# A low-half subtraction moved from VectorE to GpSimd, with the steps around it three to five picks later

## The reference, cut to what matters

```python
def chunk(xc):                                   # 128 tokens at a time
    qc = (xc @ w_query).reshape(C, PEER_HEADS, 2, half)
    s = jnp.einsum('chpd,hpnd->chpn', qc, sub_keys)
    top_s, top_i = lax.top_k(s, PEER_TOPK)       # 16 of 128, twice per head
    ...                                          # 16 of their 256 sums
    u = expert_u[expert_idx]                     # rows of 2048 floats
    vv = expert_v[expert_idx]
    act = jax.nn.gelu(jnp.einsum('chkd,cd->chk', u, xc))
    return jnp.einsum('chk,chkd->cd', (g * act).astype(vv.dtype), vv)
```

## Time and profile before

| | |
|---|---|
| median of 3 runs | 1889.43 us (1888.48 to 1889.85) |
| profiled execution | 1888.83 us, span 1887.1 us |
| PE busy | 1282.0 us (68%) |
| VectorE busy | 1343.8 us (71%) |
| ScalarE busy | 377.1 us (20%) |
| GpSimd busy | 807.5 us (43%) |
| HBM read | 631.29 MB, 337 GB/s over the span |

### The profile page before, as it was taken

How to read it: one execution, slowest core, us unless ns; L and a number is a source line. 1 busy time by engine, 2 the same in 40 slices (tenths; PEclk the granted TensorE clock), 3 DMA queues, 4 the chain that set the end, 5 groups by cost and what they waited for, 6 DMA issues and landing times.

```text
span 1887.1 us, 12624 instructions
## 1 busy us (share of the span) xinstructions
PE 1282.0 (68%) x3739; PEld 691.2 (37%) x3739; DVE 1343.8 (71%) x1811; ACT 377.1 (20%) x642; POOL 807.5 (43%) x539
## 2 busy tenths in 40 slices
PE   4799999989866667656555555655565555555567
PEld 3688887777644434211111111111121111111122
DVE  3354556355559989787787877878787787878764
ACT  3233442443422121111110101011011110101001
POOL 1000010000003655665665656666655666665654
PEclk8899999989888889877877778777777777777779
DMA  7666644415429999999999999999999999999998
GB/s 171 196 190 189 186 138 127 142 61 207 156 88 406 413 421 418 421 421 422 421 422 422 417 421 405 419 417 420 421 413 411 422 414 422 419 407 422 422 422 355
DMA packets 129230, 636.22 MB, mean 337 GB/s; under 512 B 13762, under 2 KB 22564, under 8 KB 63124
## 3 DMA queue, kind: packets, MB, share of 16 engines
q0 software_dynamic: 75136, 540.58, 70.0%
q1 hardware_dynamic: 54036, 94.95, 15.4%
HBM read 631.29 MB, written 4.19 MB: 337 GB/s over the span
## 4 chain that ended last, share of the span: by engine, by line
DMA 43%; PE 33%; DVE 8%; POOL 7%; issue 6%; ACT 2%; POOLq 0%; SPq 0%; DVEq 0%; ACTq 0%
DMA big<-in_peer_expert_v,pick_row 27%; DMA big<-in_peer_expert_u,pick_row 13%; PE ps L1443 11%; PE ps L1159 6%; PE ps L1160 6%; PE ps L1161 6%; POOL big L420 5%; DVE big L1078 3%; DMA raw<-in_w_in 2%; POOL big L415 2%; DVE split_lo L647 1%; PE ps L1226 1%; DMA raw<-in_peer_w_query 1%; PE ps L1146 1%; DVE ht L675 1%
## 5 line engine op out<-in xcount | busy, mean ns | idle before, releaser
L1443 PE MATMUL ps<-big,diag 128*128 128x512 f32 x1024 | 706.1, 828 | 491.2 <-DMA big<-in_peer_expert_v,pick_row 439.4
L1078 DVE CUSTOM_DVE_ANT_0 big<-big 128x2048 f32<-128x2048 f32 x256 | 586.2, 2291 | 212.1 <-DMA big<-in_peer_expert_u,pick_row 210.8
L420 POOL DMA_INDIRECT big<-in_peer_expert_v,pick_row x256 | 448.1, 1751 | 391.1 <-PE ps L1443 291.2
L1443 PEld LDWEIGHTS ps<-big,diag 128*128 128x128 f32 x1024 | 225.9, 243 | 960.1 <-DMA big<-in_peer_expert_v,pick_row 716.3
L415 POOL DMA_INDIRECT big<-in_peer_expert_u,pick_row x256 | 339.8, 1327 | 180.7 <-issue 70.4
L1096 DVE SCALAR_TENSOR_TENSOR big<-big,pick_w 128x1024 f32<-128x1024 f32 x256 | 327.5, 1279 | 47.8 <-DMA big<-in_peer_expert_v,pick_row 46.4
L647 DVE TENSOR_TENSOR split_lo<-raw,split_hi 128x1024 fp32r<-128x1024 f32 x152 | 185.7, 1223 | 197.8 <-ACT split_hi L444 167.6
L1159 PE MATMUL ps<-split_hi,ht 128*128 128x512 f32 x608 | 248.4, 409 | 73.9 <-DVE split_lo L647 73.9
L610 ACT ACTIVATE diag<-ident,pick_w 128x128 f32<-128x128 f32 x256 | 95.3, 395 | 808.0 <-PE ps L1443 489.1
L1160 PE MATMUL ps<-split_lo,ht 128*128 128x512 f32 x608 | 241.6, 397 | 0.0
L1161 PE MATMUL ps<-split_hi,ht 128*128 128x512 f32 x608 | 241.2, 397 | 0.0
(11 more groups left out here) (193 smaller groups left out, 677.2 us busy)
## 6 DMA issues: line engine op xcount, KB each, us to landing
raw<-in_w_in SPq DMA_DIRECT2D x88, 512.0 KB, 4.6
raw<-in_w_out SPq DMA_DIRECT2D x32, 512.0 KB, 3.5
raw<-in_peer_w_query SPq DMA_DIRECT2D x32, 512.0 KB, 11.1
raw<-in_cmp_k_w SPq DMA_DIRECT2D x8, 512.0 KB, 4.0
raw<-in_cmp_v_w SPq DMA_DIRECT2D x8, 512.0 KB, 4.1
big<-in_peer_expert_u,pick_row POOLq DMA_INDIRECT x256, 11.5
big<-in_peer_expert_v,pick_row POOLq DMA_INDIRECT x256, 11.4
big<-in_x SPq DMA_DIRECT2D x2, 1024.0 KB, 5.9
```

The source lines that it names most:

```text
L420: pool.indirect_dma_start(ring[g % RING], None, v_table, bass.IndirectOffsetOnAxis(pick_row[:, m - LAG:m - LAG + 1], 0)).then_inc(gathered ...
L1078: dve.tensor_tensor_reduce(row, row, XN[:, m // (PICKS // TT), :], 1.0, 0.0, ALU.mult, ALU.add, pick_dot[:, m:m + 1]).then_inc(dotted, 1)
L1443: ins = pe.matmul(psf[:, t * V_PE + c:t * V_PE + c + 512], diag[:, m % DIAGS, :], row[:, c:c + 512], start=k == 0, stop=k == PICKS // TT - 1)
```

## The change

GpSimd makes the low halves of query chunks 1 to 3, at k = 4 to 11, ahead of the pick's gathers. ScalarE's high halves move from k = 0..7 to 3..10, TensorE's products from 0..7 to 5..12. `to_q` moves from 9 to 13, `turn_chunk` from 10 to 13, `queries_turned` from 11 to 14, `chunk_scores` from 12 to 14 and `scores_out` from 14 to 15. The low halves of all other weights and of chunk 0 stay on VectorE.

```diff
@@ gpsimd
+            def lo(c, s):
+
+                pool.wait_ge(hi_done, SP_QUERY + c * STEPS_PER_CHUNK + s + 1)
+                pool.tensor_tensor(split_lo[:, s % SPLIT, :], raw[:, s % RAW, :], split_hi[:, s % SPLIT, :].bitcast(F32),
+                                   ALU.subtract).then_inc(split_done, 1)
+
             for m in range(STEPS):
+                n, k = divmod(m, TOPK)
+                if n + 1 < W_CHUNKS and 4 <= k < 4 + STEPS_PER_CHUNK:
+                    lo(n + 1, k - 4)
                 if m < PICKS:
                     g = u_place(m)
@@ scalar
-                    if k < STEPS_PER_CHUNK:
-                        hi_steps(c * 2 + RAW_QUERY // RAW, c * STEPS_PER_CHUNK + SP_QUERY, k, k + 1)
-                    if k == 11:
+                    if 3 <= k < 3 + STEPS_PER_CHUNK:
+                        hi_steps(c * 2 + RAW_QUERY // RAW, c * STEPS_PER_CHUNK + SP_QUERY, k - 3, k - 2)
+                    if k == 14:
                         queries_turned(c)
@@ vector
-                    if k < STEPS_PER_CHUNK:
-                        lo(k % RAW, SP_QUERY + c * STEPS_PER_CHUNK + k)
-                    if k == 9:
+                    if k == 13:
                         to_q(c)
-                    if k == 14:
+                    if k == 15:
                         scores_out(c)
@@ tensor
-                    if k < STEPS_PER_CHUNK:
-                        gemm_step([ps[:, 4 + t, :] for t in range(TT)], k % SPLIT, (2 * k, 2 * k + 1), CHUNK,
-                                  SP_QUERY + c * STEPS_PER_CHUNK + k)
-                    if k == 10:
+                    s = k - 5
+                    if 0 <= s < STEPS_PER_CHUNK:
+                        gemm_step([ps[:, 4 + t, :] for t in range(TT)], s % SPLIT, (2 * s, 2 * s + 1), CHUNK,
+                                  SP_QUERY + c * STEPS_PER_CHUNK + s)
+                    if k == 13:
                         turn_chunk(c)
-                    if k == 12:
+                    if k == 14:
                         chunk_scores(c)
```

## The result

The changed kernel takes 1961.33 us (median of 4 runs, 1960.78 to 1961.87) against 1888.95 us for the kernel before beside it: ratio 1.0386, 95% interval 1.0368 to 1.0404. It is 72 us slower. I had forecast 13 us slower and a range up to 1922 us. The profiled execution has a span of 1960.1 us, 73.0 more than before.

What follows compares the result with a forecast made beforehand. The prediction took the DMA engines to bound the pick loop, with VectorE hidden behind them. Losses of 9.0 (chunk 1) + 0 (chunk 2) + 3.8 us (chunk 3) made 12.8 us, giving 1902 us; range 1887 to 1922 us.

Steps and rivals of the forecast that it cites:

- the ceiling on any gain: Loop over the picks: DMA engines are nearly always full, so relieving an engine gives back at most 4.1 us; 0 taken.
- The duration of the subtraction: GpSimd's subtraction over 1024 columns: 2.05 us taken as two passes, with bounds of 1.1 and 3.0 us.
- The port: SBUF access: GpSimd's subtraction is shut out while VectorE works on two SBUF operands; the reverse direction not shown by rows.
- Chunk 1: Picks 4 to 11: rounds of subtraction and gather take 5.2 us, so the twelfth gather starts 9.0 us late.
- a closer coupling: ScalarE's split waits for same-pick matmuls of s - 2: 5.7 us a pick, under 6.23 in chunk 2; cost 0.
- GpSimd's round in chunks 2 and 3: Two gathers, gaps, subtraction and half a dot: 6.83 us a pick, costing 0 in chunk 2 and 3.8 us in chunk 3.
- The queue of 6.0 us as cover: In front of the DMA engines: about 6.0 us of transfers are normally queued, so GpSimd may be late by that much.
- The score steps at 0: Squeezed turn of the queries: VectorE waits some 2.3 us in chunk 1, less later, covered by queued rows; cost 0.
- The lower clock: Rival: TensorE falls to the lower clock in chunks 2 and 3, about 1947 us, or 1914 with half the picks; chance 0.07.

Runs made afterwards that it cites:

- Experiment 7: Changed kernel with products and high halves three picks earlier and GpSimd clearing the low half twice instead of subtracting: 1889.57 us, ratio 1.0007.
- experiment 2: Changed kernel, but GpSimd clears the low half twice instead of subtracting, reading nothing from SBUF, with place and wait kept: 1945.46 us, ratio 1.0308.
- experiment 3: Chunk 1 as in the changed kernel, chunks 2 and 3 as in the kernel before: 1895.37 us, ratio 1.0045.
- experiment 4: Changed kernel with products and high halves three picks earlier, GpSimd's subtractions unchanged: 1913.68 us, ratio 1.0130.
- experiment 8: All steps at the changed places, VectorE making the low halves; GpSimd only waits for the high half at the same place: 1947.52 us, ratio 1.0313.
- experiment 9: Kernel before with only the score steps at their changed later places, split and products as before: 1887.49 us, ratio 0.9997.
- experiment 1: Changed kernel with all steps at the changed places, but VectorE makes the low halves and GpSimd has no part: 1895.03 us, ratio 1.0041.
- both experiments: Changed kernel with products and high halves one pick earlier, 1928.49 us; changed kernel with GpSimd subtracting behind the pick's gathers, 1931.57 us.

## Why the prediction was wrong, point by point

- **What bounds the kernel, and the ceiling on any gain (4.1 us).** Nothing speaks against it. Experiment 7 takes 29 us of work from VectorE and gains nothing (its interval excludes a net gain over 0.05%). But its steps also stand at moved places, so that a gain of a few us could be offset there; a relief of VectorE alone was not run.
- **The duration of the subtraction.** 2.05 us taken, 2.35 measured, inside the bounds of 1.1 and 3.0. The trace now agrees within 5% with the estimate of 2.25 us that half of the 4497 ns for 2048 columns gives in the Trainium skill (GPSIMD Engine Reference, 3.1 Elementwise — side-by-side cycle accounting). The remark that GpSimd runs no plain two-input operation before the change passes over seven powers on at most 16 columns (0.69 to 3.82 us), which give no price for 1024 columns.
- **The port.** Right, and in both directions: the gathers of the earlier trace rows waited for VectorE, and now a dot of 2.29 us takes 5.07 beside a subtraction. So the Trainium skill's rule of an exclusive lock (SBUF — State Buffer, SBUF: two separate sides) holds here in the direction that the trace before could not show; clearing, which reads nothing, did not bring chunk 1's loss (experiment 2).
- **Chunk 1.** Right in mechanism and size: a round of 5.2 us forecast and 5.37 measured, the twelfth gather forecast 45.4 us after the first and measured 45.0 after it (608.50, in a loop that starts 1.9 us later), 9.0 us of loss forecast and 9.2 measured; done alone it cost 7.7 us (experiment 3).
- **The step that failed: "a closer coupling", costed at 0.** I had seen that a high half now waits for products of the same pick, and summed the work of TensorE and ScalarE in it, 5.7 us. I never asked what stands in front of those products: the add of a V row, whose landing is 8.1 us and whose gather GpSimd issues behind the very subtraction that waits for the high half. The sum was a chain, and the thing was a circle of 20.1 us that carries two picks, with longer waits for VectorE's weights at the entry of each chunk. Opening the coupling gives back 46 of the 72 us (experiment 4), and a bare wait at the same place costs 52 (experiment 8). The sum also had the adds of a pick at 0.98 us, half of the 1.96 that the earlier trace rows shows for them; with 1.96 it is 6.6 us a pick, over the 6.23 of chunk 2 but by 3.2 us in eight picks, which the 6.0 us of cover would still have brought to 0. That slip alone changed nothing.
- **GpSimd's round in chunks 2 and 3**, 6.83 us forecast. Where GpSimd doesn't wait for high halves (experiment 4) it is up to 8.6 us, since both gathers, and not half a dot on average, stand out a VectorE instruction. It costs 18 us there where I had 3.8. This term was mis-sized; the mechanism was the one given.
- **The queue of 6.0 us as cover.** It needs a GpSimd that can run ahead. In the changed kernel it is gone before the first full turn of chunk 2: the DMA share is 0.16 over 636:642 and 0.00 over 658:666.
- **The score steps at 0.** Right (experiment 9). For the split and the products at their later places 0 was wrong where VectorE subtracts, 7 us (experiment 1); what they cost in the changed kernel apart from the circle wasn't measured by itself.
- **The rivals.** The lower clock, to which I gave 0.07: one pick's add takes 3.78 us in the circle and 1.96 in the earlier trace rows, so it has a share, at most some 11 us (an estimate), but TensorE was idle first, and the turn is too long without it. Its price in the prediction, about 1947 us, rested on the same 0.98 us an add, and it is near the measured time by luck: at 3.9 us an add its pick would be 11.6 us, where the trace has 10.1 with only every second add at the lower level.

The parts: 9 (port, chunk 1) + 18 (GpSimd's round, chunks 2 and 3) + 46 (coupling) = 73 us against 72 measured. This is less of a proof than it looks: the 46 are the 72.4 less the 26.0 left in experiment 4, so the sum only says that 9 and 18 account for those 26. The parts also overlap. With the port removed first (experiment 2) only 14.6 us come back, and the coupling has 56.5 of what is left.

## What to carry to other kernels

When a step moves to the engine that issues the gathers, write down what it waits for, go back through each engine's order, and see whether you come to a gather of that same engine; then the least time per pick is the length of the circle divided by the picks in it, transfers included, and not the work that was added. It is a lower bound: with three picks in a turn both experiments took 3.5 to 6.6 us more than the range that it gave. The distance in picks is the lever: one more pick between the two ends gave back 32 us, and three gave 46. And taking 29 us of work from an engine that is busy almost all the time, but hidden behind a full DMA queue, gained nothing here.

## What the runs showed of the hardware that I had not expected

A subtraction that GpSimd begins 0.5 us after a dot's record begins still goes first: the dot recorded from 573.19 for 5.07 us contains the whole subtraction from 573.72 to 576.10, and ends 2.16 us after it. The dot of 579.24, whose record starts behind that of its subtraction (579.12), ends 2.16 us after it too. The order of the records' starts doesn't tell who has the port. And GpSimd's clearing of 1024 columns took 0.95 us beside running dots without lengthening, and a dot beside it stayed at 2.29 us: reading, not work on GpSimd as such, is what collides.
